# Query, key and value units: seven block products in place of eight, with the block sums on GpSimd

## The chip, the core and the metric

The kernel runs on one NeuronCore of a Trainium2 chip. The core has a matrix engine (TensorE, PE in the profile, with its weight loads as PEld), three engines for elementwise work (VectorE or DVE, ScalarE or ACT, GpSimd or POOL), a queue engine that mainly issues transfers (SyncE, SP) and 16 DMA engines between HBM and the on-chip memory SBUF. Matrix products are collected in eight banks of PSUM, a second on-chip memory. The metric is the device time of one execution in microseconds (us). Lower is better.

## What is computed

One layer of a streaming encoder on 512 tokens of width 1024, all in float32. The change touches the queries, keys and values:

```python
def reference(x, norm_mix_g, w_in, ...):
        xn = rmsnorm(h, norm_mix_g[l])
        proj = xn @ w_in[l]
        zu, zv, q, k, va, ga, gb = jnp.split(proj, split_idx, axis=-1)
        u = jax.nn.gelu(zu, approximate=False)
        v = jax.nn.gelu(zv, approximate=False)
        y_a = gmlp_spatial_gating(u, v, ...) @ w_branch_a[l]
        att = sliding_window_attention(q..., k..., va..., attn_sinks[l])
        y_b = att @ w_branch_b[l]
        gates = jax.nn.sigmoid(jnp.concatenate([ga, gb], axis=-1) + gate_bias[l])
        h = h + (g_a * y_a + g_b * y_b) @ w_out[l]
        hn = rmsnorm(h, norm_ffn_g[l])
        h = h + hierarchical_moe(hn, ...)
    return rmsnorm(h, norm_final_g)
```

`q` has 1024 columns, `k` and `va` 256 each: 1536 columns of `w_in`, with a contraction over 1024. Behind the attention and the gating stands a mixture of 32 experts of which each token uses two; the kernel sorts the tokens by expert and streams the weights of all experts from HBM.

## The kernel before

All weights of the first half pass through the core in 34 **units** of 1 MB (`units`). A unit is 256 columns of a weight over the whole contraction (a tall unit: 8 slices of 128 rows, `TALL`) or 512 columns over half of it (a wide unit, 4 slices, `WIDE`). Units 0 to 3 (`ZV`) are wide and give `zv`; units 4 to 9 (`Q` to `ZU`) are tall and give the queries (4 to 7), the keys (8) and the values (9); unit 10 (`ZU`) begins the next part, and the rest follows in the order of the list.

Every product is made with float32 accuracy out of three products of a rounded type (`F32R`): each operand is split in a high part and the rest, and high·high, high·low and low·high are added up in one PSUM bank (`three`, L738 to L742, `wide_unit`, L744 to L773). The path of a unit is:

1. SP issues its load to one of two buffers `raw` (L457 to L462), once the unit two places ahead has been split.
2. ACT copies the 2048 columns of `raw` to `whi` (`split_hi`, L1351 to L1355), two buffers as well. It waits until PE has finished with the unit whose `whi` it overwrites (`wait_unit_used`).
3. DVE subtracts `whi` from `raw` and writes `wlo` (`split_lo`, L1698).
4. PE works through the unit. A tall unit has two tiles (`tall_tile`, L810): 128 columns of the weight are the stationary operand, all 512 tokens of the activation `xnT_hi` or `xnT_lo` the moving one, 8 slices by three products, so 24 matmuls of 128x512 for a tile and 48 for a unit.
5. ACT copies each finished tile out of PSUM to `qT`, `kT` or `vaT` (L1446 to L1449).

The splits run one unit ahead of PE. Each engine has an instruction stream of its own that is written out by hand in the code and is carried out in its order; the streams meet at semaphores (`hi_split`, `lo_split`, `act_tile_done` and others). An instruction that waits holds up all that is behind it in its stream. In the query, key and value units DVE has, besides the splits, the layernorm of `v_tok`: the statistics of all four token tiles and an inverse root in unit 4 (`layernorm_stats`), then one tile in each of units 4 to 7 (`layernorm`). `v_tok` is read by PE behind the first tiles of unit 10. In the wide units DVE also makes the position biases `alibi` (L1708 to L1717) and turned weights `wsT`. GpSimd does nothing between the start (`ident`, `dist_i`) and the end of the attention.

Behind the first half the expert weights are loaded in place of buffers that PE has finished with; SP waits for PE or DVE before each of these loads.

## Time and profile before

| | |
|---|---|
| Time, median of 3 runs | 893.21 us |
| Lowest and highest of them | 892.12 and 893.25 us |
| The profiled execution's own time | 892.7 us |
| Its span, first to last instruction | 890.8 us |
| PE busy | 840.9 us, 94% of the span |
| DVE busy | 418.4 us, 47% |
| ACT busy | 238.4 us, 27% |
| POOL busy | 7.0 us, 1% |
| Mean granted TensorE clock | 0.981 |
| Query, key and value units | 59.1 to 124.4 us |

All rows come from one profiled execution; its time is 0.5 us below the median of the three runs. A row of a timeline gives the start from the span's first instruction, the duration, engine and line, what is written and read, the shape, and in brackets how long the engine was idle just before and for whom. Matmuls are pipelined: a duration covers also the way through the array, and what one costs in a dense stream is the distance from its start to the next one's. The same holds, to a smaller degree, for DVE and ACT: a row of 0.68 us may be followed by the next one 0.60 us after its start. "PEclk" is the share of the full TensorE clock that was granted.

### The profile page before, as it was taken

Reading aid. Unit: us, or ns where it says so; the run is one execution under the profiler, and the core shown is the slowest. Engines: PE = TensorE matmul, PEld = TensorE weight load, DVE = VectorE, ACT = ScalarE, POOL = GpSimd, SP = SyncE. Lnnn points to the kernel's source line nnn. Section 1 sums busy time; section 2 is a strip of 40 time slices with the busy share of each in tenths; the row PEclk is TensorE's granted clock in tenths of the full one; section 3 lists DMA queues with packets and bytes.
Section 4 is the critical chain, followed back from the end, with each engine's and each line's share of the span. In section 5 each row is a group of like instructions: output and inputs, shape, how many; then the busy total and the mean of one; then the engine's idle time right before and its main releaser. Section 6 shows DMA issues by size and latency. Waiting matters only on the chain.

```text
span 890.8 us, 11444 instructions
## 1 busy us (share of the span) xinstructions
PE 840.9 (94%) x4631; PEld 550.5 (62%) x4631; DVE 418.4 (47%) x814; ACT 238.4 (27%) x439; POOL 7.0 (1%) x24
## 2 busy tenths in 40 slices
PE   8999999999999999999999969999995699999985
PEld 7888888887877888888734333544532353644632
DVE  5538326777765344433868245135133224335134
ACT  6332222465453222224414211110110100100114
POOL 0000000000000100000000000000000000000000
PEclk9999999999999999999999989999996899999998
DMA  8544312212123733796899999999999999999994
GB/s 295 147 94 108 103 59 94 96 48 95 61 83 78 214 95 95 264 402 235 349 379 390 415 430 425 428 426 430 424 429 427 426 428 428 427 427 426 427 410 182
DMA packets 71751, 249.49 MB, mean 280 GB/s; under 512 B 23016, under 2 KB 46608, under 8 KB 58512
## 3 DMA queue, kind: packets, MB, share of 16 engines
q1 hardware_dynamic: 71328, 247.66, 71.5%
q0 software_dynamic: 288, 1.05, 0.3%
q8 instruction: 38, 0.62, 0.3%
q14 instruction: 17, 0.14, 0.0%
q10 hardware_dynamic: 80, 0.02, 0.0%
HBM read 244.51 MB, written 4.20 MB: 279 GB/s over the span
## 4 chain that ended last, share of the span: by engine, by line
PE 85%; DMA 11%; DVE 2%; ACT 1%; issue 1%; SPq 0%; DVEq 0%; POOL 0%; ACTq 0%; POOLq 0%
PE bank L1065 17%; PE bank L740 10%; PE bank L742 10%; PE bank L741 10%; PE bank L1124 8%; DMA R<-w_down 6%; DMA R<-w_up 3%; PE bank L769 2%; PE bank L768 2%; PE bank L767 2%; DMA R<-w_gate 2%; PE bank L1029 2%; PE by_side L1029 2%; PE bank L1152 2%; PE bank L1111 2%; PE bank L1153 1%
## 5 line engine op out<-in xcount | busy, mean ns | idle before, releaser
L1065 PE MATMUL bank<-R,packT 128*64 128x512 f32 (+1 forms) x972 | 184.4, 603 | 15.3 <-DMA R<-w_up 12.8
L1065 PEld LDWEIGHTS bank<-R,packT 128*64 128x64 f32 (+1 forms) x972 | 58.3, 128 | 123.4 <-issue 122.9
L1698 DVE TENSOR_TENSOR wlo<-raw,whi 128x2048 fp32r<-128x2048 f32 x33 | 75.5, 2288 | 84.8 <-ACT whi L1355 84.7
L740 PE MATMUL bank<-xnT_hi,whi 128*128 128x512 f32 x288 | 113.2, 393 | 0.0
L742 PE MATMUL bank<-xnT_hi,wlo 128*128 128x512 f32 x288 | 112.1, 389 | 0.0
L741 PE MATMUL bank<-xnT_lo,whi 128*128 128x512 f32 x288 | 112.1, 389 | 0.0
L1124 PE MATMUL bank<-R,actT 128*64 128x512 f32 (+1 forms) x384 | 74.8, 640 | 14.9 <-DMA R<-w_down 14.7
L1355 ACT ACTIVATE whi<-raw 128x2048 fp32r<-128x2048 f32 x33 | 63.1, 1912 | 67.4 <-PE by_side L742 33.8
L740 PEld LDWEIGHTS bank<-xnT_hi,whi 128*128 128x128 f32 x288 | 54.1, 188 | 11.4 <-issue 0.6
L742 PEld LDWEIGHTS bank<-xnT_hi,wlo 128*128 128x128 f32 x288 | 54.1, 188 | 11.3
L1124 PEld LDWEIGHTS bank<-R,actT 128*64 128x64 f32 (+1 forms) x384 | 22.7, 135 | 62.0 <-issue 61.3
L741 PEld LDWEIGHTS bank<-xnT_lo,whi 128*128 128x128 f32 x288 | 54.1, 188 | 10.9
L2196 DVE SCALAR_TENSOR_TENSOR y_lo<-bank,small,y_hi 128x512 fp32r<-128x512 f32 x26 | 19.3, 750 | 82.3 <-ACT y_hi L1573 82.3
L2205 DVE TENSOR_TENSOR h_tok<-bank,h_tok 128x512 f32<-128x512 f32 x84 | 52.1, 676 | 6.9 <-PE bank L1153 6.9
L1573 ACT ACTIVATE y_hi<-bank,small 128x512 fp32r<-128x512 f32 x26 | 17.8, 690 | 107.0 <-PE bank L1124 91.7
L2182 DVE TENSOR_REDUCE small<-bank 128x1 f32<-128x512 f32 x13 | 9.0, 690 | 72.1 <-PE bank L1082 72.0
L2188 DVE TENSOR_TENSOR act_rows<-silu_g,bank 128x512 f32<-128x512 f32 x13 | 14.0, 1078 | 60.8 <-PE bank L1065 60.8
L1568 ACT ACTIVATE actT<-by_side 128x512 f32<-128x512 f32 x13 | 7.8, 600 | 119.0 <-PE by_side L1089 119.0
L1152 PE MATMUL bank<-y_hi,onehotT 128*128 128x512 f32 x84 | 35.0, 417 | 1.5 <-ACT packT L1554 1.5
L1153 PE MATMUL bank<-y_lo,onehotT 128*128 128x512 f32 x84 | 33.0, 392 | 0.0
L1382 ACT ACTIVATE probs<-probs,small 128x128 f32<-128x128 f32 (+1 forms) x64 | 24.4, 386 | 23.1 <-DVE small L1766 23.1
L1560 ACT ACTIVATE silu_g<-bank 128x512 f32<-128x512 f32 x12 | 7.1, 596 | 82.5 <-PE bank L1065 82.5
(418 smaller groups left out, 1323.4 us busy)
## 6 DMA issues: line engine op xcount, KB each, us to landing
R<-w_up SPq DMA_DIRECT2D x27, 2048.0 KB, 20.7
R<-w_gate SPq DMA_DIRECT2D x25, 2048.0 KB, 22.5
R<-w_down SPq DMA_DIRECT2D x21, 2048.0 KB, 24.4
raw<-w_in SPq DMA_DIRECT2D x17, 1024.0 KB, 5.1
R<-w_down SPq DMA_DIRECT2D x12, 1024.0 KB, 14.2
R<-w_gate SPq DMA_DIRECT2D x14, 512.0 KB, 8.5
raw<-w_in SPq DMA_DIRECT2D x20, 256.0 KB, 4.6
R<-w_up SPq DMA_DIRECT2D x5, 1024.0 KB, 8.3
```

The source lines that it names most:

```text
L740: pe.matmul(dst, hi_w, hi_x, start=start, stop=False)
L741: pe.matmul(dst, hi_w, lo_x, start=False, stop=False)
L742: return pe.matmul(dst, lo_w, hi_x, start=False, stop=stop)
L1029: mm = pe.matmul(bank[PACK_BANKS[c // 2]][:, (c % 2) * 2 * P:(c % 2 + 1) * 2 * P], part[:, t, c, :], onehot[:, t, :], start=(t == 0 and pa ...
L1065: mm = pe.matmul(dst[s * w:(s + 1) * w, :], packT[:, side, c, s * w:(s + 1) * w], part_of(s, c) if part_of else slots[s // 2].tiles[s % 2] ...
L1124: mm = pe.matmul(bank[5 + n][s * w:(s + 1) * w, :], actT[:, c, s * w:(s + 1) * w], slots[s // 2].tiles[s % 2][:, c * D + n * 512:c * D + ( ...
L1152: pe.matmul(dst, onehotT[odd][:, t * P:(t + 1) * P], y_hi[:, n * 512:(n + 1) * 512], start=True, stop=False)
L1153: pe.matmul(dst, onehotT[odd][:, t * P:(t + 1) * P], y_lo[:, n * 512:(n + 1) * 512], start=False, stop=True).then_inc(line.spread_done, 1)
L1355: act.activation(whi[c % 2][:, :], raw[c % 2][:, :], ACT.Copy).then_inc(hi_split, 1)
L1382: act.activation(row, row, ACT.Exp, bias=neg_max[s % 2][:, r:r + 1], accum_out=denom[s % 2][:, r:r + 1])
L1698: dve.tensor_tensor(wlo[c % 2][:, :], raw[c % 2][:, :], whi[c % 2][:, :].bitcast(F32), ALU.subtract).then_inc(lo_split, 1)
L2205: dve.tensor_tensor(part, bank[spread_banks(line, i)[n][t]][:, :], part, ALU.add).then_inc(line.h_added, 1)
```

## The change

The six units 4 to 9 are computed by the Winograd form of Strassen's identity, with a two by two partition of each product: the 1024 deep contraction is halved (4 slices each), the unit's 256 columns are two halves of 128, and the 512 tokens two halves of 256. In place of eight block products of 128 columns by 4 slices by 256 tokens there are seven (`seventh`), on sums of blocks. A block is 12 matmuls of 128x256; a unit has 84 of them (`seven_unit`), the six units 504, where 288 of 128x512 stood.

- **Sums of the activation**: `tT_sum` 0, 1 and 3 are made once by GpSimd in seven additions or subtractions of 128x1024, one behind the other; `tT_sum` 2 by DVE in three. ACT and DVE split the four of them (`tT_hi`, `tT_lo`).
- **Sums of the weights**: for each unit GpSimd makes four sums of 128x512 (`s_sum`), in order s1 to s4, as soon as the unit is loaded. For units from the third on they also wait until the unit two ahead is split.
- **Splits**: in place of one split of 2048 columns there are seven of 512 (`high_block` on ACT, `low_block` on DVE), three of them of blocks of `raw` and four of sums. They go to a ring of eight places made of the same `whi` and `wlo`; block q waits until PE has finished block q - 8. The last two have places of their own (`late_hi`, `late_lo`). SP loads a unit once all seven blocks of the one two ahead are split.
- **Results**: partial sums in PSUM serve two or more results. ACT copies three of them out of PSUM (`keep`), DVE makes three quarters of the result by adding a kept part to a bank (`add_corner`), ACT copies the fourth. Block 2 of a unit waits for the first copy of ACT, block 4 for the third, block 6 for the second `add_corner` of DVE.
- **Order**: the layernorm statistics are made in units 0 and 1 of the six (two token tiles each, the inverse root in unit 1), the layernorm's four tiles in units 2 to 5. The split of unit 10 stands in unit 5.

The rest is renumbering of waits, and semaphores that are merged (`pool_made`, `small_ready`).

```diff
+        RAW_BLOCK = {0: (0, 0), 3: (0, 1), 6: (1, 1)}
+        SUM_BLOCK = {1: 0, 2: 1, 4: 2, 5: 3}
...
+        def block_home(u, b, ring, late):
+            q = 7 * u + b
+            home = late[q - BLOCKS + 2][:, :] if q >= BLOCKS - 2 else ring[q % 8 // 4][:, q % 4 * 512:(q % 4 + 1) * 512]
+            return home.rearrange("p (k n) -> p k n", k=4)
...
             def load_unit(c):
                 if c >= 2:
-                    sp.wait_ge(hi_split, c - 1)
-                    sp.wait_ge(lo_split, c - 1)
+                    sp.wait_ge(hi_split, units_split(c - 2))
+                    sp.wait_ge(lo_split, units_split(c - 2))
                 for dst, src in units[c]:
...
+            pool.wait_ge(xnT_ready, X_READY)
+            minus(t1, hi(0, 1), hi(0, 0)).then_inc(pool_made, 1)
+            minus(tT_part[0][:, :, :], lo(0, 1), lo(0, 0)).then_inc(pool_made, 1)
+            pool.wait_ge(pool_made, T_SUMS + 2)
+            pool.tensor_tensor(t1, t1, tT_part[0][:, :, :], ALU.add).then_inc(pool_made, 1)
...
+            for u in range(SEVENS):
+                c = Q + u
+                if u == 1:
+                    pool.wait_ge(xnT_ready, X_READY + 3 + 4)
+                pool.wait_ge(unit_loaded[c % 2], landed[c])
+                if u >= 2:
+                    pool.wait_ge(lo_split, Q + 7 * (u - 1))
+                s1, s2, s3, s4 = (tile[:, :, :] for tile in s_sum[u % 2])
+                pool.tensor_tensor(s1, raw_block(c, 1, 0), raw_block(c, 1, 1), ALU.add).then_inc(pool_made, 1)
+                pool.wait_ge(pool_made, S_SUMS + 4 * u + 1)
+                minus(s2, s1, raw_block(c, 0, 0)).then_inc(pool_made, 1)
+                minus(s3, raw_block(c, 0, 0), raw_block(c, 1, 0)).then_inc(pool_made, 1)
+                pool.wait_ge(pool_made, S_SUMS + 4 * u + 2)
+                minus(s4, raw_block(c, 0, 1), s2).then_inc(pool_made, 1)
...
-            for c in range(Q, ZU):
-                for m in range(2):
-                    act_tile(c, m, 8 + 2 * (c - Q) + m)
+            def seventh(u, b, dst, x_hi, x_lo, start):
+
+                pe.wait_ge(lo_split, Q + 7 * u + b + 1)
+                w_h, w_l = block_home(u, b, whi, late_hi), block_home(u, b, wlo, late_lo)
+                for k in range(4):
+                    pe.matmul(dst, w_h[:, k, :], x_hi[:, k, :], start=start and k == 0, stop=False, skip_group_check=True)
+                    pe.matmul(dst, w_h[:, k, :], x_lo[:, k, :], start=False, stop=False, skip_group_check=True)
+                    mm = pe.matmul(dst, w_l[:, k, :], x_hi[:, k, :], start=False, stop=k == 3, skip_group_check=True)
+                mm.then_inc(act_tile_done, 1)
+
+            def seven_unit(u):
+
+                main_psum, first_psum, fifth_psum = (bank[2 * i + u % 2][:, 0:2 * P] for i in range(3))
+                if u < 2:
+                    pe.wait_ge(act_tile_read, 5 + u)
+                else:
+                    pe.wait_ge(act_tile_read, 8 + 2 * (u - 1))
+                    pe.wait_ge(corner_ready, 3 * (u - 1))
+                seventh(u, 0, main_psum, x_block(xnT_hi, 0, 0), x_block(xnT_lo, 0, 0), True)
+                pe.wait_ge(xnT_ready, X_READY + 3 + 1)
+                seventh(u, 1, fifth_psum, tT_hi[0], tT_lo[0], True)
+                pe.wait_ge(part_kept, 3 * u + 1)
+                pe.wait_ge(xnT_ready, X_READY + 3 + 2)
+                seventh(u, 2, main_psum, tT_hi[1], tT_lo[1], False)
+                if u < 2:
+                    pe.wait_ge(act_tile_read, 7 + u)
+                seventh(u, 3, first_psum, x_block(xnT_hi, 1, 0), x_block(xnT_lo, 1, 0), True)
+                pe.wait_ge(part_kept, 3 * u + 3)
+                pe.wait_ge(xnT_ready, X_READY + 3 + 3)
+                seventh(u, 4, main_psum, tT_hi[2], tT_lo[2], False)
+                seventh(u, 5, fifth_psum, x_block(xnT_hi, 1, 1), x_block(xnT_lo, 1, 1), False)
+                pe.wait_ge(corner_ready, 3 * u + 2)
+                pe.wait_ge(xnT_ready, X_READY + 3 + 4)
+                seventh(u, 6, main_psum, tT_hi[3], tT_lo[3], False)
+
+            for u in range(SEVENS):
+                seven_unit(u)
...
+            def high_block(u, b):
+                q = 7 * u + b
+                if q < 4:
+                    wait_unit_used(act, 2)
+                elif q < 8:
+                    act.wait_ge(act_tile_done, 8)
+                elif q < BLOCKS - 2:
+                    act.wait_ge(act_tile_done, 8 + q - 7)
+                if b in RAW_BLOCK:
+                    act.wait_ge(unit_loaded[u % 2], landed[Q + u])
+                else:
+                    act.wait_ge(pool_made, S_SUMS + 4 * u + SUM_BLOCK[b] + 1)
+                act.activation(block_home(u, b, whi, late_hi), block_source(u, b), ACT.Copy).then_inc(hi_split, 1)
+
+            def keep(u, i, b, src):
+                act.wait_ge(act_tile_done, 8 + 7 * u + b + 1)
+                return act.activation(kept[u % 2][i][:, :], src[:, 0:2 * P], ACT.Copy)
...
+                if c == Q - 1:
+                    high_t(0, pool_made, T_SUMS + 3)
+                    high_t(1, pool_made, T_SUMS + 5)
+                    high_t(2, xnT_ready, X_READY + 3)
+                    for b in range(4):
+                        high_block(0, b)
...
+            high_block(0, 4)
+            high_block(0, 5)
+            high_t(3, pool_made, T_SUMS + 7)
+            high_block(0, 6)
+            act.wait_ge(wsT_psum, 1)
+            for u in range(SEVENS):
+                last = u == SEVENS - 1
+                main_psum, fifth_psum = bank[u % 2], bank[4 + u % 2]
+                if not last:
+                    high_block(u + 1, 0)
+                keep(u, 0, 0, main_psum).then_inc(part_kept, 1)
+                if last:
+                    split_hi(ZU)
+                else:
+                    high_block(u + 1, 1)
+                keep(u, 1, 1, fifth_psum).then_inc(part_kept, 1)
+                if not last:
+                    high_block(u + 1, 2)
+                keep(u, 2, 2, main_psum).then_inc(part_kept, 1)
+                if not last:
+                    for b in range(3, 7):
+                        high_block(u + 1, b)
+                act.wait_ge(act_tile_done, 8 + 7 * u + 7)
+                act.activation(corner(u, 1, 0), main_psum[:, 0:2 * P], ACT.Copy).then_inc(act_tile_read, 2)
...
+            def low_block(u, b):
+                dve.wait_ge(hi_split, Q + 7 * u + b + 1)
+                lo = dve.tensor_tensor(block_home(u, b, wlo, late_lo), block_source(u, b),
+                                       block_home(u, b, whi, late_hi).bitcast(F32), ALU.subtract)
+                lo.then_inc(lo_split, 1)
+
+            def add_corner(u, m, h, b, src, i):
+                dve.wait_ge(act_tile_done, 8 + 7 * u + b + 1)
+                dve.wait_ge(part_kept, 3 * u + i + 1)
+                dve.tensor_tensor(corner(u, m, h), src[:, 0:2 * P], kept[u % 2][i][:, :], ALU.add).then_inc(corner_ready, 1)
...
+                if c == Q - 1:
+                    for i in range(3):
+                        low_t(i)
+                    for b in range(6):
+                        low_block(0, b)
+                    low_t(3)
+                    low_block(0, 6)
...
+            for u in range(SEVENS):
+                last = u == SEVENS - 1
+                main_psum, first_psum, fifth_psum = bank[u % 2], bank[2 + u % 2], bank[4 + u % 2]
+                if not last:
+                    low_block(u + 1, 0)
+                    low_block(u + 1, 1)
+                else:
+                    split_lo(ZU)
+                if u < 2:
+                    layernorm_stats(2 * u)
+                else:
+                    layernorm(u - 2)
+                if not last:
+                    low_block(u + 1, 2)
+                    low_block(u + 1, 3)
+                add_corner(u, 0, 0, 3, first_psum, 0)
+                if not last:
+                    low_block(u + 1, 4)
+                add_corner(u, 1, 1, 4, main_psum, 1)
+                if not last:
+                    low_block(u + 1, 5)
+                add_corner(u, 0, 1, 5, fifth_psum, 2)
+                if not last:
+                    low_block(u + 1, 6)
```

The orders of the built programs show it at four places. First TensorE in a middle unit: before, triples of 128x512 with the normed activation `xnT` as moving operand.

```order
L742 MATMUL bank<-xnT_hi,wlo_75 128x512
L740 MATMUL bank<-xnT_hi,whi_73 128x512
L741 MATMUL bank<-xnT_lo,whi_73 128x512
L742 MATMUL bank<-xnT_hi,wlo_75 128x512
L740 MATMUL bank<-xnT_hi,whi_73 128x512
```

Now the end of one block and the beginning of the next, with the sums of activations (`tT`) in place of `xnT`.

```order
L972 MATMUL by_side<-tT_hi_93,whi_73 128x256
L973 MATMUL by_side<-tT_lo_97,whi_73 128x256
L974 MATMUL by_side<-tT_hi_93,wlo_75 128x256
L972 MATMUL bank<-tT_hi_94,whi_73 128x256
L973 MATMUL bank<-tT_lo_98,whi_73 128x256
L974 MATMUL bank<-tT_hi_94,wlo_75 128x256
```

Each matmul has half the columns, and the bank changes behind 12 of them.

Second ScalarE, from the end of the wide units on; `v_tok` is the Gelu of the tiles of `zv`, `whi` a high part, `qT` a result. Before:

```order
L1436 ACTIVATE v_tok<-bank 128x512 x3
L1436 ACTIVATE v_tok<-by_side 128x512
L1355 ACTIVATE whi_73<-raw_71 128x2048
L1449 ACTIVATE qT<-bank 128x512 x2
L1355 ACTIVATE whi_72<-raw_70 128x2048
```

And now, in the piece that begins three instructions behind those Gelus (the high parts of blocks 4 and 5 stand between):

```order
L1543 ACTIVATE tT_hi_96<-tT_sum_104 128x1024
L1557 ACTIVATE whi_73<-raw_70 128x512
L1557 ACTIVATE whi_73<-raw_71 128x512
L1561 ACTIVATE kept_115<-bank 128x256
L1557 ACTIVATE whi_72<-s_sum_111 128x512
L1561 ACTIVATE kept_116<-by_side 128x256
L1557 ACTIVATE whi_72<-s_sum_112 128x512
L1561 ACTIVATE kept_117<-bank 128x256
```

The first copy of a partial sum (`kept_115`) stands behind the remaining splits of unit 0 and the first one of unit 1.

Third VectorE in its layernorm work. Before, with the split of a whole unit between two tiles:

```order
L1733 TENSOR_SCALAR v_tok<-v_tok,small 128x1024
L1734 TENSOR_TENSOR v_tok<-v_tok,ln_g 128x1024
L1735 TENSOR_TENSOR v_tok<-v_tok,ln_b 128x1024
L1698 TENSOR_TENSOR wlo_74<-raw_70,whi_72 128x2048
L1733 TENSOR_SCALAR v_tok<-v_tok,small 128x1024
```

Now, unit 2 of the six (`qT<-bank,kept_116` is the addition that block 6 waits for):

```order
L1983 TENSOR_TENSOR wlo_75<-s_sum_111,whi_73 128x512
L1886 TENSOR_SCALAR v_tok<-v_tok,small 128x1024
L1887 TENSOR_TENSOR v_tok<-v_tok,ln_g 128x1024
L1888 TENSOR_TENSOR v_tok<-v_tok,ln_b 128x1024
L1983 TENSOR_TENSOR wlo_75<-s_sum_112,whi_73 128x512
L1983 TENSOR_TENSOR wlo_74<-raw_71,whi_72 128x512
L1990 TENSOR_TENSOR qT<-bank,kept_115 128x256
L1983 TENSOR_TENSOR wlo_74<-s_sum_113,whi_72 128x512
L1990 TENSOR_TENSOR qT<-bank,kept_116 128x256
```

The addition on which PE waits stands behind a layernorm tile, three splits and another addition. In unit 1 the statistics of two tiles and the inverse root stand where the layernorm tile is here.

Fourth GpSimd behind `dist_i`; before, its next work was `row_iota`, behind the attention.

```order
L704 IOTA dist_i 128x128
L707 TENSOR_TENSOR tT_sum_101<-xnT_hi 128x1024
L707 TENSOR_TENSOR tT_part_105<-xnT_lo 128x1024
L715 TENSOR_TENSOR tT_sum_101<-tT_sum_101,tT_part_105 128x1024
L707 TENSOR_TENSOR tT_sum_102<-xnT_hi,tT_sum_101 128x1024
L719 TENSOR_TENSOR tT_sum_102<-tT_sum_102,xnT_lo 128x1024
L707 TENSOR_TENSOR tT_sum_104<-xnT_hi,tT_sum_102 128x1024
L723 TENSOR_TENSOR tT_sum_104<-tT_sum_104,xnT_lo 128x1024
L732 TENSOR_TENSOR s_sum_107<-raw_70 128x512
```

Seven instructions of 128x1024 and 24 of 128x512 stand where there was nothing.

## Rows read from the trace of the kernel before

**Rows 1.** The page: the chain that ended last, by engine.

```profile
PE 85%; DMA 11%; DVE 2%; ACT 1%; issue 1%; SPq 0%; DVEq 0%; POOL 0%; ACTq 0%; POOLq 0%
```

**Rows 2.** Busy time by stretch: the six units (columns: PE, PEld, DVE, ACT, POOL).

```profile
59.12:124.40 65.28, 65.28 (x290) 54.07 (x288) 34.32 (x42) 18.00 (x18) 0.00 (x0) 1.00 0.33 97
```

**Rows 3.** Timeline of PE: first matmuls of unit 4 and of unit 10.

```profile
59.12 0.39 PE L740 MATMUL bank<-xnT_hi,whi 128*128 128x512 f32 x1
...
124.40 0.39 PE L740 MATMUL bank<-xnT_hi,whi 128*128 128x512 f32 x1
```

**Rows 4.** Timeline of PE: second and last of 64 matmuls of 128x256 (`gather_rows`).

```profile
565.41 0.28 PE L1029 MATMUL bank<-onehot,hn_lo 128*128 128x256 f32 x1
...
572.84 0.28 PE L1029 MATMUL by_side<-onehot,hn_lo 128*128 128x256 f32 x1
```

**Rows 5.** Timeline of ACT: copies by size, the last Gelu of `zv`.

```profile
4.48 1.06 ACT L1391 ACTIVATE xn_tok<-x_tok 128x1024 f32<-128x1024 f32 x1 [0.51 <-DMA x_tok<-x]
...
7.23 2.57 ACT L1401 ACTIVATE whi<-raw 128x512 fp32r<-128x512 f32 x4
10.30 0.47 ACT L1407 ACTIVATE xnT_hi<-by_side,small 128x256 fp32r<-128x256 f32 x1 [0.49 <-PE bank L725]
...
59.32 0.60 ACT L1436 ACTIVATE v_tok<-by_side 128x512 f32<-128x512 f32 x1 [2.12 <-PE by_side L769]
```

**Rows 6.** Timeline of DVE: low parts of 256 and 512 columns.

```profile
10.81 0.48 DVE L1801 SCALAR_TENSOR_TENSOR xnT_lo<-by_side,small,xnT_hi 128x256 fp32r<-128x256 f32 x1 [0.72 <-ACT xnT_hi L1407]
11.21 0.68 DVE L1795 TENSOR_TENSOR wlo<-raw,whi 128x512 fp32r<-128x512 f32 x1
11.81 0.48 DVE L1801 SCALAR_TENSOR_TENSOR xnT_lo<-bank,small,xnT_hi 128x256 fp32r<-128x256 f32 x1
```

**Rows 7.** Timeline of DVE: statistics, inverse root and one tile of the layernorm.

```profile
67.08 1.29 DVE L1724 BATCH_NORM_STATS2 small<-v_tok 128x6 f32<-128x512 f32 x2
...
70.21 0.17 DVE L1728 COPY small<-small 128x4 f32<-128x4 f32 x1
...
72.60 0.81 DVE L1733 TENSOR_SCALAR v_tok<-v_tok,small 128x1024 f32<-128x1024 f32 x1
...
75.85 2.28 DVE L1698 TENSOR_TENSOR wlo<-raw,whi 128x2048 fp32r<-128x2048 f32 x1
```

**Rows 8.** Timelines of POOL and DVE around 291 us.

```profile
291.38 1.40 POOL L683 TENSOR_SCALAR_AFFINE_SELECT earlier<-all_ones 128x128 bf16<-128x128 bf16 x1
...
290.33 2.29 DVE L1698 TENSOR_TENSOR wlo<-raw,whi 128x2048 fp32r<-128x2048 f32 x1 [0.53 <-ACT whi L1355]
```

**Rows 9.** POOL by form: a read with DVE idle, and iotas of two sizes.

```profile
L658 POOL TENSOR_SCALAR_AFFINE_SELECT ident<-ident 128x128 f32<-128x128 f32 x1 | 0.3, 287 | 0.2 <-POOL ident L656 0.2
...
L664 POOL IOTA row_iota<- 128x256 f32 x1 | 0.4, 351 | 288.1 <-DVE attT_lo L1775 288.1
...
L661 POOL IOTA dist_i<- 128x128 int32 x1 | 0.2, 230 | 0.0
```

**Rows 10.** Timeline of DVE from 27 us; timeline of PE at wide unit 2.

```profile
27.98 2.97 DVE L1715 TENSOR_SCALAR alibi<-dist 64x128 f32<-64x128 f32 x16
...
31.19 2.29 DVE L1698 TENSOR_TENSOR wlo<-raw,whi 128x2048 fp32r<-128x2048 f32 x1
...
37.26 0.48 PE L767 MATMUL bank<-whi,xnT_hi 128*128 128x512 f32 x1
```

**Rows 11.** Timeline of PE: two waits and the work behind them, then the granted clock.

```profile
446.45 0.64 PE L1065 MATMUL bank<-gate_fifth,packT 128*64 128x512 f32 x1 [1.35 <-DVE packT L2213]
...
678.48 9.03 PE L1065 MATMUL bank<-R,packT 128*32 128x512 f32 x64 [11.91 <-DMA R<-w_up]
...
444.00:446.00 2.00, 1.11 (x6) 1.00 0.02 6
678.00:680.00 2.00, 1.52 (x8) 0.50 0.98 418
```

**Rows 12.** A wait of the SP queue in front of expert weights' loads.

```profile
SPq L526 <- PE by_side L769: 25.3, 1, 25.3
```

133 lines of the change are left out of this document (87 added, 46 removed).

## The prediction

> **What bounds the kernel now.** I read the chain that ended last first: PE is 85% of it and DVE 2% [rows 1], so what counts is whether PE is given work. The busy times by stretch say the same of the six units: from 59.12 to 124.40 PE is busy for all of the 65.28 us, DVE for 34.32, ACT for 18.00, POOL for none, and the granted clock is 1.00 [rows 2]. The reader is to see there that the stage is dense on PE, and that the other engines run beside it with room. Units 4 to 9 cost 124.40 - 59.12 = 65.28 us on the path, 10.88 a unit, 65.28 / 288 = 0.2267 us for a matmul of 512 columns [rows 3]. Later loads wait for PE or DVE [rows 12]: no transfer of the expert weights starts at a fixed time, each follows a buffer that was finished with. So what is won or lost before 124.4 us is carried to the end one to one.
>
> **What is removed and added on PE.** Removed are 288 x 0.2267 = 65.3 us. Added are 504 matmuls of 256 columns. The trace has such a stream: 62 distances from 565.41 to 572.84 are 7.43 us, 0.120 each [rows 4], with a weight load of 128 columns before each of them as in the new code. That is 504 x 0.120 = 60.5 us, 10.08 a unit, 1.44 a block. PE's own work shrinks by **4.8 us**. It is not half of 0.2267 because each matmul has some 0.013 us that do not shrink (0.120 x 2 - 0.2267).
>
> **What the other engines now have to do in 10.08 us.** Prices: ACT, high part of 512 columns 2.57 / 4 = 0.64, of 1024 columns 1.06, a copy of 256 out of PSUM 0.47 [rows 5]. DVE, low part of 512 columns 0.60 (11.21 to 11.81), an operation on 256 columns with a bank 0.40, or 0.48 to its end [rows 6]; statistics of two token tiles 70.21 - 67.08 = 3.13; inverse root 72.60 - 70.21 = 2.39; a layernorm tile 75.85 - 72.60 = 3.25 [rows 7]. ACT has 7 x 0.64 + 4 x 0.47 = 6.4 us a unit, and fits. DVE has 7 x 0.60 + 3 x 0.40 = 5.4, with a layernorm tile 8.7, with statistics and root 10.9. The sum of a unit fits in most of them, but PE waits in the middle: block 6 is due 6 x 1.44 = 8.64 us into a unit and needs DVE's second addition, and the order puts the layernorm before it. I lay the streams side by side, counting from the unit's start on PE; a block's result is there 0.16 after its end (0.28 - 0.12 in [rows 4]).
>
> - Units 2 to 4. DVE can begin the low part of the next unit's block 1 at 2.8: block 0 ends at 1.44 + 0.16, ACT then keeps its copy and makes the high part. From there low part 0.60, layernorm 3.25, two low parts 1.20, addition 0.40, low part 0.60, addition 0.48: done at 9.3. PE waits 0.65 in each of the three: **2.0 us**.
> - Unit 1. In place of 3.25 stand 3.13 + 2.39 = 5.52: **2.9 us**.
> - Unit 5. No low parts of a next unit, but the whole split of unit 10: ACT ends its high part at 4.0, DVE 2.20, layernorm 3.25, two additions 0.88: done at 10.3, **1.7 us**.
> - Unit 0. Its first copy stands on ACT behind the last Gelu (starts at 59.32 [rows 5]), four high parts of 512 and one of 1024: 0.54 + 4 x 0.62 + 1.0 + 0.47 = 4.5, so 63.8 where block 2 is due at 59.12 + 2.88 = 62.0: 1.9 us (0.62 being the distance of starts). Then DVE, which gets its low parts late by that, has 3.13 of statistics in its chain and is 2.2 late for blocks 4 and 6: **4.1 us** in all.
>
> These waits are 2.0 + 2.9 + 1.7 + 4.1 = 10.7 us. They swallow the 4.8: **+5.9 us** before GpSimd has cost anything.
>
> **GpSimd.** No row of before shows a two-input operation of it. From below its price is DVE's for the same shape, 0.60 for 512 columns [rows 6]. From above, its one-input select of 128x128, 0.287 us, four times: 1.15, and 2.3 for 1024 [rows 9]. From the two iotas, 0.23 and 0.351, a column costs 0.95 ns and the start 0.11; with two reads for a write I take twice that slope, 1.1 for 512 and 2.1 to 2.2 for 1024, near the upper end, since the select reads as well and an iota does not. By itself this hides: seven sums from 27.2 end at 43, unit 4's four at 47, and ACT wants the first of them only when PE is through with the `whi` of wide unit 2, at 37.3 + 48 x 0.2267 = 48.2 [rows 10]. The question is what happens when both engines read SBUF.
>
> There the trace has one row that decides for me. The select at 291.38 took 1.40 us, where its like took 0.29; a DVE split with two SBUF inputs ran from 290.33 to 292.62, in its usual 2.29, and the select ended just behind it [rows 8, 9]. So the GpSimd read stood still until DVE's instruction was through. Bounds for the cost of this: nothing, if DVE always goes first and GpSimd's work fits in the gaps; or every GpSimd instruction in front of a DVE instruction, the full price each time. I take turns: who asks waits for the one that runs, then they alternate. In unit 1 two of GpSimd's four sums come into DVE's chain, 2 x 1.1 = 2.2. In unit 0 two come into it, and the start is 1 us later since the seven sums, held up by DVE's work between 31 and 48, end near 49: 3.1. In units 2 to 4 the sums start late in the unit, as the load waits for the seven splits two units ahead, so some two of 1.1 fall into the chain in all three: 2.3. Sum 7.6 us.
>
> The Trainium skill, page "SBUF — State Buffer", section "Who interferes with whom", says that a DVE instruction with two SBUF inputs contends with a GpSimd one that reads SBUF, and that the first to issue keeps the shared ports for its whole instruction. By that rule, which also speaks against the change, the waits on DVE's side are as real as the one in [rows 8], which agrees with it on GpSimd's side; no row of before shows DVE waiting. The skill's "GPSIMD Engine Reference", section 3.1, gives 4497 ns for an addition of 2048 columns; a quarter of it, 1.12 us, is an estimate for a weight sum, and the sum above would be the same by it.
>
> **Clock.** Behind a wait of 1.35 us the granted clock stays 1.00, behind one of 11.91 it is 0.50 [rows 11], and the 64 matmuls there take 9.03 us where the same 64 take some 7.1. The waits here reach 4 to 5 us, between the two, so 0 to 2 us; I take 1.
>
> **Sum**, against the profiled execution's 892.7: -4.8 + 10.7 + 7.6 + 1 = +14.5, so 907.2; the median of the runs is 0.5 above that execution: **907.7 us**.
>
> **Rivals.**
> 1. *GpSimd costs DVE nothing* (DVE always goes first, or the two only share). For it: the DVE split in [rows 8] was not lengthened. Against it: there DVE had begun first. Then -4.8 + 10.7: 892.7 + 5.9 + 0.5 = **899.1**.
> 2. *The turns begin at once.* At 27.15 DVE enters a run of some 20 short operations on the biases, ahead of the split of unit 2 [rows 10], and GpSimd gets its seven long sums at the same moment. If each short one has to let a sum of 2.2 pass, the split that ends at 33.5 now ends at 33.5 + 7 x 2.2 = 48.9, and PE, which wants it at 37.3, waits 11.5 us. Against it: those operations have one input, and no row tells whether such a one meets GpSimd. Saved is little, since the later sums are then early. Sum 907.7 + 11.5 = **919**, with the clock's second us 920.
> 3. *The other side: the waits do not come.* It decides where DVE's second addition is done before 8.64. In units 2 to 4 that takes 0.65 us less of chain, in unit 1 2.9 less, for instance if DVE's starts come closer than the rows say and it enters each unit with its low parts already made. Then PE keeps its 4.8: 893.2 - 4.8 = **888.4**. Against it: all prices are of this trace, and the low part of block 1 cannot be made before block 0 of the running unit has left the ring. A half of it gives no change.
> 4. *The matmuls of 256 columns do not run at 0.120*, since each needs a load of new weights, which takes 0.19 in the rows of PEld. [Rows 4] has a new load each time too. It would cost up to 504 x 0.07 = 35 us; I give it 2 in 100.
>
> **Chances.** Forecast 0.48 (turns with another rule of precedence move it between 904 and 914), rival 1 0.20, rival 2 0.20, rival 3 0.07, no change 0.03, rival 4 0.02. The range goes from rival 1 with a us to spare, 898, to rival 2 at 920. A difference of 0.2% is 1.8 us, about what a measurement of this kernel tells from no change: faster 0.07, same 0.03, slower 0.90.
>
> **What will show it.** In the profile after: distances of 0.120 us between PE's new matmuls in dense stretches; block 6 idle for DVE's addition in every unit, longest in units 0 and 1; block 2 of unit 0 idle for ACT's copy. Rows of 128x512 low parts that take 1 us and more while GpSimd's sums run would show the turns, and unchanged 0.68 us would speak for rival 1. PE idle before unit 2 of the wide ones would be rival 2. Unit 10 should start near 138 us; from there all should be as before, later by the same amount. I am wrong if GpSimd's sums of 512 columns are far from 1.1 us, or if the expert stage takes up the delay.

## The result: 42 us slower, three times the forecast

| | before | after |
|---|---|---|
| Median of 4 runs each | 893.23 us | 935.44 us |
| Lowest and highest | 892.12, 893.50 | 934.51, 935.75 |
| Span of the profiled execution | 890.8 us | 933.8 us |
| First matmul of unit 4 (seven unit 0) | 59.12 us | 72.62 us |
| First matmul of unit 10 | 124.40 us | 166.3 us |
| First matmul of the expert stage | 441.5 us | 483.4 us |

The ratio is 1.0477, 95% interval 1.0464 to 1.0489. The forecast was 907.7 in 898 to 920: the sign was right, the size not. Unit 10 and the expert stage are both 41.9 us late and the span is 43.0 longer, so the loss arises before 166 us and is carried on, as the prediction had it.

The page of after, busy times and the chain that ended last. Against [rows 1] PE fell from 85% of the chain to 74% and DVE rose from 2% to 10%:

```profile
PE 852.3 (91%) x4847; PEld 567.3 (61%) x4847; DVE 481.2 (52%) x875; ACT 256.3 (27%) x491; POOL 65.1 (7%) x55
...
PE 74%; DMA 11%; DVE 10%; issue 2%; ACT 2%; SPq 0%; DVEq 0%; ACTq 0%
```

The stretch that answers to [rows 2] (columns: PE, PEld, DVE, ACT, POOL busy, then the granted clock). PE works for 71 of 94 us, at 0.87 of its clock, where it was busy throughout at 1.00:

```profile
72.62:166.32 93.70, 71.14 (x506) 69.51 (x505) 71.15 (x94) 33.18 (x64) 33.10 (x20) 0.87 0.29 79
```

Timeline of PE in after: the first two of the new matmuls, 0.12 apart as in [rows 4], and then all rows up to unit 10 that have a wait above 1 us. The first wait stands before wide unit 2, where [rows 10] has a start at 37.26:

```profile
72.62 0.28 PE L972 MATMUL bank<-xnT_hi,whi 128*128 128x256 f32 x1
72.74 0.28 PE L973 MATMUL bank<-xnT_lo,whi 128*128 128x256 f32 x1
...
48.09 0.79 PE L843 MATMUL bank<-whi,xnT_hi 128*128 128x512 f32 x1 [10.71 <-DVE wlo L1849]
...
76.77 0.38 PE L972 MATMUL bank<-tT_hi,whi 128*128 128x256 f32 x1 [1.11 <-ACT kept L1561]
...
81.17 0.39 PE L972 MATMUL bank<-tT_hi,whi 128*128 128x256 f32 x1 [1.27 <-ACT kept L1561]
...
88.13 0.58 PE L972 MATMUL bank<-tT_hi,whi 128*128 128x256 f32 x1 [3.83 <-DVE qT L1990]
...
106.51 0.58 PE L972 MATMUL bank<-tT_hi,whi 128*128 128x256 f32 x1 [6.65 <-DVE qT L1990]
...
123.28 0.58 PE L972 MATMUL bank<-tT_hi,whi 128*128 128x256 f32 x1 [4.13 <-DVE qT L1990]
...
140.21 0.58 PE L972 MATMUL bank<-tT_hi,whi 128*128 128x256 f32 x1 [4.15 <-DVE qT L1990]
...
164.79 0.38 PE L972 MATMUL bank<-tT_hi,late_hi 128*128 128x256 f32 x1 [1.31 <-DVE vaT L1990]
```

The rows of 3.83, 6.65, 4.13 and 4.15 us are block 6 of units 0 to 3, waiting for DVE's second addition. From one of them to the next is one unit, 10.08 us without losses: 106.51 - 88.13 = 18.38 = 10.08 + 6.65 + 1.65, and 123.28 - 106.51 = 16.77 = 10.08 + 4.13 + 2.56. The third part is 0.16 of refilling and otherwise the clock, which the windows show (last columns: granted clock, DMA, GB/s). It reads 1.00 in the first part of the wait, 0.74 from 104 to 106, where PE is still idle, and 0.50 to 0.55 from 106 to 112:

```profile
100.00:104.00 4.00, 0.00 (x0) 0.00 (x0) 3.73 (x9) 0.52 (x1) 2.86 (x3) 1.00 0.00 0
104.00:108.00 4.00, 1.49 (x7) 1.49 (x8) 3.98 (x8) 0.00 (x0) 0.00 (x0) 0.62 0.00 0
108.00:112.00 4.00, 4.00 (x21) 4.00 (x21) 0.69 (x1) 0.91 (x2) 0.00 (x0) 0.53 0.70 222
```

The balance up to unit 10: matmuls -4.8; start 13.5 (72.62 - 59.12: 10.7 of wait, 2.7 of half clock behind it); waits in the units 1.11 + 1.27 + 3.83 + 6.65 + 4.13 + 4.15 + 1.31 and a quarter us in unit 4 = 22.7, with 0.16 of refilling for each (0.28 of duration less 0.12 of distance, [rows 4]) some 1.2 more; half clock behind the four long ones 1.5 + 2.4 + 2.6 + 2.6 = 9.1. The sum is 41.7 of the 41.9.

What DVE and GpSimd did at the start, timelines of after. Against [rows 10], the sixteen multiplications of the biases (`alibi`) take 13.37 us in place of 2.97, and two short operations ahead of them 2.40 each, the length of one of GpSimd's sums. Of the sixteen only five are held, one for each sum that is still to come (2.27 to 2.38 us); the one behind each of these, and all six behind the last sum, take 0.21 to 0.23. So the delay is as long as the sums that run, not one sum for every short operation. The split for wide unit 2 begins at 45.74 in place of 31.19:

```profile
27.26 2.40 DVE L1860 TENSOR_SCALAR dist<-dist 64x128 f32<-64x128 f32 x1
29.69 2.40 DVE L1861 SCALAR_TENSOR_TENSOR dist<-dist 128x128 f32<-128x128 f32 x1
32.13 13.37 DVE L1866 TENSOR_SCALAR alibi<-dist 64x128 f32<-64x128 f32 x16
...
45.74 2.29 DVE L1849 TENSOR_TENSOR wlo<-raw,whi 128x2048 fp32r<-128x2048 f32 x1
...
27.18 2.40 POOL L707 TENSOR_TENSOR tT_sum<-xnT_hi 128x1024 f32<-128x1024 f32 x1 [25.46 <-DVE xnT_lo L1973]
...
41.82 2.34 POOL L723 TENSOR_TENSOR tT_sum<-tT_sum,xnT_lo 128x1024 f32<-128x1024 f32 x1
```

The same in unit 1, where DVE makes the inverse root out of operations on four columns. Those that fall beside one of GpSimd's sums (97.74 to 102.86, 1.26 to 1.30 each) take 1.14 to 1.29 us, their likes 0.16. The statistics (BATCH_NORM_STATS2) are not held: those at 80.59 and 82.14, beside sums too, kept 1.27 and 1.29.

```profile
97.57 0.17 DVE L1837 TENSOR_SCALAR small<-small 128x4 f32<-128x4 f32 x1
97.77 1.29 DVE L1838 TENSOR_SCALAR small<-small 128x4 int32<-128x4 int32 x1
99.10 0.16 DVE L1841 TENSOR_TENSOR small<-small 128x4 f32<-128x4 f32 x1
99.30 1.14 DVE L1842 SCALAR_TENSOR_TENSOR small<-small 128x4 f32<-128x4 f32 x1
...
97.74 1.30 POOL L732 TENSOR_TENSOR s_sum<-raw 128x512 f32<-128x512 f32 x1 [7.18 <-DMA raw<-w_in]
99.12 1.30 POOL L707 TENSOR_TENSOR s_sum<-s_sum,raw 128x512 f32<-128x512 f32 x1
```

Low parts of 512 columns take 1.4 to 1.8 us where they meet a sum, 0.68 where not. Unit 2 has, ahead of the addition on which block 6 waits, a pass of the layernorm and three low parts that are held:

```profile
115.65 2.20 DVE L1888 TENSOR_TENSOR v_tok<-v_tok,ln_b 128x1024 f32<-128x1024 f32 x1
117.78 1.78 DVE L1983 TENSOR_TENSOR wlo<-s_sum,whi 128x512 fp32r<-128x512 f32 x1
119.48 1.75 DVE L1983 TENSOR_TENSOR wlo<-raw,whi 128x512 fp32r<-128x512 f32 x1
...
121.48 1.41 DVE L1983 TENSOR_TENSOR wlo<-s_sum,whi 128x512 fp32r<-128x512 f32 x1
```

Over their lengths alone (1.23 and 0.68) that is 3.9 us.

### The profile page after: what moved, and what is told of

Read it like the earlier page. It is cut to its first block, busy times and chain, and to the rows that moved or that the text cites. A ratio compares the mean times of both kernels' runs of the same rounds, so it can differ in the third digit from the quotient of the medians.

```text
span 933.8 us, 12110 instructions
## 1 busy us (share of the span) xinstructions
PE 852.3 (91%) x4847; PEld 567.3 (61%) x4847; DVE 481.2 (52%) x875; ACT 256.3 (27%) x491; POOL 65.1 (7%) x55
## 3 DMA queue, kind: packets, MB, share of 16 engines
q0 software_dynamic: 288, 1.05, 0.3%
## 4 chain that ended last, share of the span: by engine, by line
PE 74%; DMA 11%; DVE 10%; issue 2%; ACT 2%; SPq 0%; DVEq 0%; ACTq 0%
PE bank L1176 16%; PE bank L816 7%; PE bank L817 7%; PE bank L818 7%; PE bank L1235 6%; DMA R<-w_down 5%; DMA R<-w_gate 3%; DMA R<-w_up 3%; PE bank L843 2%; PE bank L844 2%; PE bank L845 2%; PE bank L1140 2%; PE by_side L1140 2%; DVE wlo L1983 2%; PE bank L1222 2%
## 5 line engine op out<-in xcount | busy, mean ns | idle before, releaser
L1849 DVE TENSOR_TENSOR wlo<-raw,whi 128x2048 fp32r<-128x2048 f32 x27 | 61.8, 2287 | 49.6 <-ACT whi L1466 49.6
L816 PE MATMUL bank<-xnT_hi,whi 128*128 128x512 f32 x192 | 75.9, 395 | 0.0
L818 PE MATMUL bank<-xnT_hi,wlo 128*128 128x512 f32 x192 | 74.8, 390 | 0.0
L817 PE MATMUL bank<-xnT_lo,whi 128*128 128x512 f32 x192 | 74.8, 389 | 0.0
L1466 ACT ACTIVATE whi<-raw 128x2048 fp32r<-128x2048 f32 x27 | 51.6, 1911 | 60.3 <-PE by_side L818 33.8
L1235 PEld LDWEIGHTS bank<-R,actT 128*64 128x64 f32 (+1 forms) x384 | 22.7, 135 | 61.0 <-issue 60.3
L972 PE MATMUL bank<-tT_hi,whi 128*128 128x256 f32 x80 | 25.8, 323 | 21.2 <-DVE qT L1990 18.8
L816 PEld LDWEIGHTS bank<-xnT_hi,whi 128*128 128x128 f32 x192 | 36.1, 188 | 7.6 <-issue 0.6
L818 PEld LDWEIGHTS bank<-xnT_hi,wlo 128*128 128x128 f32 x192 | 36.0, 188 | 7.6
L817 PEld LDWEIGHTS bank<-xnT_lo,whi 128*128 128x128 f32 x192 | 36.1, 188 | 7.0
L972 PEld LDWEIGHTS bank<-tT_hi,whi 128*128 128x128 f32 x80 | 17.5, 219 | 22.7 <-DVE qT L1990 19.6
```

What stands on the lines that cost most here:

```text
L816: pe.matmul(dst, hi_w, hi_x, start=start, stop=False)
L817: pe.matmul(dst, hi_w, lo_x, start=False, stop=False)
L818: return pe.matmul(dst, lo_w, hi_x, start=False, stop=stop)
L972: pe.matmul(dst, w_h[:, k, :], x_hi[:, k, :], start=start and k == 0, stop=False, skip_group_check=True)
L1235: mm = pe.matmul(bank[5 + n][s * w:(s + 1) * w, :], actT[:, c, s * w:(s + 1) * w], slots[s // 2].tiles[s % 2][:, c * D + n * 512:c * D + ( ...
L1466: act.activation(whi[c % 2][:, :], raw[c % 2][:, :], ACT.Copy).then_inc(hi_split, 1)
```

## The experiments

The theory after this reading (A): an instruction of GpSimd and one of DVE take turns, one whole instruction each, short ones of DVE too. Against it stood that the delays come from the change's longer instruction lists, from their order, or from the placing of the data.

### 1. The same sums in the kernel before

In the kernel before, seven additions whose results nothing uses:

```diff
+            pool.wait_ge(xnT_ready, WIDE + KT)
+            for n in range(7):
+                pool.wait_ge(iota_made, n + 1)
+                pool.tensor_tensor(spare.rearrange("p (k n) -> p k n", k=4), xnT_hi[:, 0:4, 0:256].bitcast(F32),
+                                   xnT_lo[:, 0:4, 0:256].bitcast(F32), ALU.add).then_inc(iota_made, 1)
```

> The kernel before, with seven two-input additions of 128x1024 float32 added on GpSimd behind the normalised activation (from 27 us), whose results nothing uses; the matmuls and all else are those of before. Theory A (turns): VectorE's sixteen alibi multiplications take 13 us in place of 2.97, TensorE waits 10 to 11 us for the low part of unit 2 and runs 2 to 3 us at half clock after it: 893.2 + 13.5 = 906.7, range 904 to 908. Theory B (the delay belongs to something else in the change): 893.2, within 1.

Measured: 906.99 us (905.74 to 907.96, ratio 1.0153, interval 1.0136 to 1.0171), +14.1. The timelines of DVE and PE, and a window, have the rows of after again, in a kernel in which nothing else of DVE's and PE's work is changed; the second row is the summary of the sixteen (ns: shortest, median, longest):

```profile
32.26 13.37 DVE L1722 TENSOR_SCALAR alibi<-dist 64x128 f32<-64x128 f32 x16
...
L1722 DVE TENSOR_SCALAR alibi<-dist x16: 209/220/2372, 32.3 to 45.4; 64x128 f32<-64x128 f32 x16
...
48.21 0.80 PE L774 MATMUL bank<-whi,xnT_hi 128*128 128x512 f32 x1 [10.82 <-DVE wlo L1705]
...
50.00:54.00 4.00, 4.00 (x11) 3.05 (x10) 2.30 (x2) 0.00 (x0) 0.00 (x0) 0.50 1.28 238
```

Theory A holds for the start in the time and in the cause: 14 us of the 42 are seven sums of GpSimd that meet a run of short operations. Its turns are not strictly one for one: the median of the sixteen is 0.22, so most of them pass unheld.

### 2. Instructions that only write

The same place, but fourteen iotas of 1024 columns into the spare tile (`pool.iota` for `pool.tensor_tensor` above).

> The kernel before, with fourteen instructions on GpSimd that only write 128x1024 float32 (ascending numbers, no input from memory) in the same place, from 27 us, whose results nothing uses. Theory A1 (the turns are for reading two operands): no alibi row above 0.3 us, 893.2 within 1. Theory A2 (any GpSimd instruction that touches the core's memory takes turns with VectorE): sixteen alibi multiplications at one GpSimd instruction each; with instructions of 1 us or more these take at least 12 us, and the time is above 902.

Measured: 897.76 us (894.41 to 899.25), ratio 1.0060. Neither expectation is right. Timelines of GpSimd and DVE:

```profile
27.10 14.72 POOL L668 IOTA spare<- 128x1024 f32 x14 [25.38 <-DVE xnT_lo L1827]
...
27.20 0.97 DVE L1716 TENSOR_SCALAR dist<-dist 64x128 f32<-64x128 f32 x1
28.20 0.29 DVE L1717 SCALAR_TENSOR_TENSOR dist<-dist 128x128 f32<-128x128 f32 x1
28.53 8.16 DVE L1722 TENSOR_SCALAR alibi<-dist 64x128 f32<-64x128 f32 x16
...
37.66 2.29 DVE L1705 TENSOR_TENSOR wlo<-raw,whi 128x2048 fp32r<-128x2048 f32 x1
```

The multiplications with one input are held by an instruction that only writes (8.16 us in place of 2.97, an iota being 14.72 / 14 = 1.05). They pass in pairs, one pair for each iota, and a single one lasts 0.62 to 0.98; the second expectation had put one iota to each of the sixteen. The operations with two inputs, L1717 and the split, are not: 0.29 and 2.29, their usual lengths. Beside sums L1717's like took 2.40 (L1861 in after). So a two-input operation of DVE meets GpSimd's reads, and a one-input TENSOR_SCALAR also its writes. The profiled execution had a wait of 2.70 us on PE and the clock at 1.00 behind it, at 894.4; two of the other runs took 899, and why is open.

### 3. Which of DVE's instructions are held

In the kernel before, fourteen sums as in the first experiment, but from 134 us on (`pool.wait_ge(gate_used, 1)`), where DVE gates the tiles of the next stage.

> The kernel before, with fourteen additions of 128x1024 float32 on GpSimd whose results nothing uses, beginning when VectorE has used the first gate (near 134.5 us, in the matmuls of unit 10), where VectorE's rows have several kinds of operands: gated from a bank of PSUM and the biases (0.69 us), gated from two tiles (0.69), a one-input cast (0.43), the low part (0.69), the split of a unit (2.28). Theory A (turns, whole instructions; and by the trace of the changed kernel instructions with an operand in PSUM are not held): the rows with an operand in PSUM stay at 0.69, the other four kinds take up to 2.4 us more each while the sums run; the sums are 14 x 2.35 = 33 us of which VectorE's idle time (5.6 of 12.7 us for two tiles) takes in some 20, so that TensorE waits some 13 us for the gated tiles, with 2 to 5 us of half clock: 905 to 912. Theory D (only the many short instructions at 27 us are held, longer ones are not): all these rows keep their length, 893.

Measured: 907.63 us (906.21 to 908.69), as theory A has it, with three waits of PE (3.44, 6.01, 1.03), though for the splits and not for gated tiles. DVE's rows from 134.79, each one beside sums:

```profile
134.79 2.76 DVE L1874 TENSOR_TENSOR spT_lo<-gated,spT_hi 128x512 fp32r<-128x512 f32 x1
137.48 4.45 DVE L1705 TENSOR_TENSOR wlo<-raw,whi 128x2048 fp32r<-128x2048 f32 x1
141.85 0.68 DVE L1868 TENSOR_TENSOR gated<-bank,gate_bs 128x512 f32<-128x512 f32 x1
142.56 2.14 DVE L1871 TENSOR_TENSOR gated<-gbuf,gated 128x512 f32<-128x512 f32 x1
144.74 2.50 DVE L1873 CAST spT_hi<-gated 128x512 fp32r<-128x512 f32 x1
...
134.38 41.28 POOL L668 TENSOR_TENSOR spare<-xnT_hi,xnT_lo 128x1024 f32<-128x1024 f32 x14 [132.66 <-DVE gated L1871]
```

The addition with one operand in PSUM keeps its 0.68. The others, of 0.69, 2.29, 0.69 and 0.43 us alone, take 1.45 to 2.16 us more each, at most one sum. The sums pay too: 41.28 / 14 = 2.95 in place of 2.35.

The Trainium skill, page "SBUF — State Buffer", section "Who interferes with whom", has these cases: two SBUF inputs contend with a GpSimd instruction that reads, not with one that only writes; a copy, cast or `tensor_scalar` can contend in a mode with two ports; one SBUF input outside these modes does not. The rows of this and the last experiment agree with it, and so do the statistics above; which mode an instruction ran in no row shows. The prediction took from that section only the part on two inputs; the part on `tensor_scalar` speaks for its rival 2.

### 4. The changed kernel with later activation sums

```diff
             pool.wait_ge(xnT_ready, X_READY)
+            pool.wait_ge(lo_split, units_split(2))
```

> The changed kernel with one wait more: GpSimd begins its seven 1024-column sums of the activation only when VectorE has split unit 2, so that they run from about 34 to 51 us, behind VectorE's sixteen alibi multiplications and not beside them. Theory A (an instruction of GpSimd that reads two operands and an instruction of VectorE take turns, one whole instruction each): the 16 alibi rows take 2.97 us in place of 13.37, TensorE's unit 2 begins near 37.3 and not 48.1, and the 10.8 us of wait and the 2.7 us of half clock behind it go: 935.4 - 13.5 = 921.9, range 920 to 926 since the sums now end nearer to their use. Theory B (VectorE is late for another reason that the change brought, as its own longer list of work or another placing of the tiles): the alibi rows stay at 13.37 us and the time stays at 935.4, within 1.

Measured: 926.19 us (924.12 to 927.46), just above theory A's range and far from theory B. The biases are back at 2.97 us, and PE does not wait before wide unit 2. But only 9.2 of the 13.5 us are won. The sums now meet other work of DVE, and PE begins seven unit 0 with a wait (timelines of DVE and PE):

```profile
43.33 3.41 DVE L2001 TENSOR_TENSOR tT_sum<-xnT_hi 128x1024 f32<-128x1024 f32 x1
...
63.05 0.55 PE L973 MATMUL bank<-xnT_hi,whi 128*128 128x256 f32 x1 [3.36 <-DVE wlo L1984]
```

### 5. Without weight sums, and without any sums

Two kernels that leave sums out. In the first the weights' sums are missing from the kernel of experiment 4, in the second all of GpSimd's sums from the changed kernel (one-element writes stand in their place). Neither computes the layer any more.

```diff
-                pool.tensor_tensor(s1, raw_block(c, 1, 0), raw_block(c, 1, 1), ALU.add).then_inc(pool_made, 1)
-                minus(s2, s1, raw_block(c, 0, 0)).then_inc(pool_made, 1)
...
+                for s in (s1, s2, s3, s4):
+                    pool.memset(s[:, 0:1, 0:1], 0.0).then_inc(pool_made, 1)
```

> The kernel late_sums with the weights' block sums (128x512, four a unit) left out and the activation's (128x1024) kept, so the output is not that of the reference. It parts what late_sums still loses: the wait of 3.4 us at unit 0's beginning, with its half clock, belongs to the activation's sums, which keep VectorE's three own sums at 3.4 in place of 1.22 us; the waits in units 0 to 3 to the weights' sums. Then: no_sums 898.3 + 3.4 + 1.5 = 903, range 900 to 906. If the waits in the units came from elsewhere than these sums, 915 or more.

Measured: 897.74 us (896.91 to 899.18). The weights' sums are worth 926.2 - 897.7 = 28.5 us. My expectation was 5 too high, and the time lies below its range, because I had put the wait at 63 us to the activation's sums. It is gone here, though these are still made and DVE's own sums still take 3.4 us each: what had delayed the first low parts were the weights' sums from 55.65 on.

> The changed kernel with GpSimd's sums left out: each of its instructions of sums writes one element only, and the splits read a tile of the activation or of the raw weights where a sum stood; every other instruction (504 matmuls of 256 columns, copies, splits, additions, their order and waits) is unchanged, so the output is not that of the reference. Theory A (turns between GpSimd and VectorE): all that is left is the shorter matmuls, -4.8, and the waits that ScalarE's and VectorE's orders make without GpSimd, +10.7, with 1 to 3 us of clock: 893.2 - 4.8 + 10.7 + 1 to 3 = 900 to 902; no VectorE row of 512 columns above 0.70 us. Theory C (the waits of the seven-product units come from the order of VectorE's instructions alone, GpSimd only moved the start): the start is cured, 13.5 us, and the rest stays: 921.9.

Measured: 898.34 us (898.08 to 898.93), ratio 1.0060, a little under the 900 to 902 of theory A and far from theory C. So the sums on GpSimd cost 935.4 - 898.3 = 37.1 us: 14.1 at the start (experiment 1), and the rest, 23.0, in the units. This division holds for the changed kernel only: with the start cured, the weights' sums alone were worth 28.5. What remains is the change without its sums, still 5.5 us slower than before. Timeline of PE, its waits above 1 us:

```profile
63.14 0.39 PE L963 MATMUL bank<-tT_hi,whi 128*128 128x256 f32 x1 [1.11 <-ACT kept L1552]
...
70.50 0.39 PE L963 MATMUL bank<-tT_hi,whi 128*128 128x256 f32 x1 [1.34 <-DVE qT L1981]
...
83.34 0.38 PE L963 MATMUL bank<-tT_hi,whi 128*128 128x256 f32 x1 [2.51 <-DVE qT L1981]
```

With 1.31 in unit 5 and 0.24 twice, PE waits 6.7 us, 7.7 with refilling, and runs at 0.60 of its clock from 84 to 88 us; unit 10 begins at 129.4, 5.0 later than before: -4.8 + 7.7 + some 2 of clock.

Leaving the sums out takes away two things, the turns and the time in which a split waits for its sum. The rows of after tell them apart. Ahead of block 6 of units 1, 2 and 3 DVE's held operations are 4.2, 3.9 and 4.0 us longer than their likes. PE's waits there exceed this kernel's (2.51, none and 0.24) by nearly the same: 4.1, 4.1 and 3.9. So in these units it is the turns.

### 6. The order of DVE's work

DVE's layernorm pieces go behind the three additions of each unit, in three kernels: that of experiment 4, the one without sums, and the changed one.

```diff
             for u in range(SEVENS):
...
-                if u < 2:
-                    layernorm_stats(2 * u)
-                else:
-                    layernorm(u - 2)
...
                 if not last:
                     low_block(u + 1, 6)
+                if u < 2:
+                    layernorm_stats(2 * u)
+                else:
+                    layernorm(u - 2)
```

> The kernel late_sums, with VectorE's layernorm pieces (statistics, inverse root, the three passes over the token rows) moved in each unit from before the three additions to behind them. In late_sums TensorE waits 3.8, 6.5, 4.1 and 4.1 us in units 0 to 3 for the second addition. Theory O (order: the addition is late because it stands behind the layernorm piece in VectorE's queue): these waits fall below 1 us each, and with the half clock behind them some 25 us go: below 905. Theory W (work: VectorE's and GpSimd's own two-operand work may not overlap, and a unit's 7 splits of 0.68, 3 additions of 0.41, 4 sums of 1.27 and 3.3 us of layernorm are 14.4 us against 10.1 us of matmuls): the order only decides which unit pays; over six units some 74 us stand against 60.5 and what VectorE is ahead by, so at least 10 us of wait stay, now also for low parts, with half clock: 914 to 926.

Measured: 906.37 us (905.99 to 910.16), 19.8 less than in the old order, and just above theory O's bound. Theory W is wrong that order only moves the waits about, and its 914 was too high. The six units now take 137.0 - 62.4 = 74.6 us. That meets its 74 us of shared work by luck: some 5 of them are half clock, DVE stands idle for 5 of the last 34, and in the kernel `reordered` below the units take 145.7 - 72.8 = 72.9. In the old order they took 157.5 - 63.05 = 94.5, because PE waited for additions that stood behind work without a deadline. Of the four waits for the second addition one long one is left, where theory O had all below 1 us (timeline of PE):

```profile
71.98 0.39 PE L973 MATMUL bank<-tT_hi,whi 128*128 128x256 f32 x1 [2.09 <-ACT kept L1562]
...
103.04 0.58 PE L973 MATMUL bank<-tT_hi,whi 128*128 128x256 f32 x1 [5.64 <-DVE qT L1991]
```

> The changed kernel with one thing moved: VectorE's layernorm pieces stand behind the three additions of each unit and no longer before them; GpSimd's sums begin at 27 us as in the change. Theory O (order, from the pair late_sums and late_reordered, 926.2 to 906.4): the start keeps its 10.8 us of wait and 2.7 us of half clock, the waits for the second addition in units 0 to 3 go down from 18.8 us by some 13 and the half clock behind them by some 6: 935.4 - 19.8 = 915.6, range 913 to 919. If the gain of late_reordered came from VectorE being ahead because the start was cured, little comes here: above 925.

Measured: 915.85 us (915.67 to 916.50), as theory O had it from the pair before. So of the change's 42 us almost 20 go by moving four lines, with the sums where they were.

> The kernel no_sums (GpSimd's sums left out, the splits read other data, so the output is not that of the reference), with VectorE's layernorm pieces behind the three additions of each unit. In no_sums TensorE still waits 1.3 and 2.5 us for the second addition in units 0 and 1, 0.2 twice, with about 1.7 us of half clock; that is order, if the order theory holds where nothing is shared: 898.3 - 1.3 - 2.5 - 0.5 - 1.7 - 0.6 = 891.7, range 890 to 893, a gain of 1 to 3 us on the kernel before, which is what seven products would bring if the sums were free. If the waits there are of another kind (ScalarE's copies late), it stays at 898.

Measured: 890.28 us (median of 11, 889.87 to 891.78), ratio 0.9978, interval 0.9969 to 0.9987. Two waits are left, 1.11 and 0.57; unit 10 begins at 121.6: -4.8 + 1.7 + 0.3 = -2.8. By the medians the gain is 2.0 us. That is what seven products give when GpSimd's sums are free.

Between the two reordered kernels, 906.4 and 890.3, lie 16 us that GpSimd's sums cost in this order. They are not shown to be a floor. The wait of 5.64 stands behind two tiles of statistics and the inverse root in one piece (89.0 to 98.2, four of its small operations held), ahead of unit 2's low parts, and no run with GpSimd's sums spreads that piece.

### 7. The sums on VectorE

GpSimd makes no sums. DVE makes them all; the biases move behind unit 10, the layernorm behind the additions and is written with two passes for three.

```diff
+                    s_sums(u + 1, 0)
                     low_block(u + 1, 1)
+                    s_sums(u + 1, 1)
...
+                then(dve.scalar_tensor_tensor(out=row, in0=row, scalar=ln_mv[:, 2 * t:2 * t + 1], in1=ln_g[:, :],
+                                              op0=ALU.subtract, op1=ALU.mult))
+                dve.scalar_tensor_tensor(out=row, in0=row, scalar=rstd[:, t:t + 1], in1=ln_b[:, :], op0=ALU.mult,
+                                         op1=ALU.add).then_inc(ln_ready, 1)
```

> The changed kernel with all block sums on VectorE and none on GpSimd (seven more of 128x1024 at 1.22 us and four of 128x512 at 0.68 us in each unit), the alibi multiplications moved behind the gating of unit 11, the layernorm's three passes written as two (2.46 in place of 3.27 us a token tile) and moved behind the additions, three of its four tiles to the end of unit 5. If only sharing with GpSimd was dear, VectorE holds: 7 splits, 4 sums and 3 additions are 8.7 us of a unit's 10.1: -4.8 of matmuls, +1.3 for ScalarE's copy in unit 0, +1.3 at unit 5's end: 891, range 889.5 to 893. If VectorE becomes the bound instead (its 32 us before unit 0 are full, and the layernorm has to end by 7 us into unit 10), TensorE waits for low parts or the layernorm: 895 to 905.

Measured: 895.89 us (894.96 to 897.17), ratio 1.0035, in the range of the second case, but by one long wait and not by DVE as the bound throughout. One wait made most of the difference to the first case, and the window behind its start shows the clock (timeline of PE, window):

```profile
101.36 0.58 PE L939 MATMUL bank<-tT_hi,whi 128*128 128x256 f32 x1 [2.75 <-ACT kept L1528]
...
100.00:104.00 4.00, 2.64 (x12) 2.64 (x13) 3.97 (x8) 2.34 (x6) 0.00 (x0) 0.59 0.02 4
```

ACT's copy was late since it stands behind a high part, which waited for a sum, which stood on DVE behind 5.5 us of statistics and inverse root in one piece (92.7 to 98.2). The next kernel spreads these pieces. It also makes ACT's first copy of unit 0 earlier, each unit's first two sums before its first low part, and one layernorm tile before the split of unit 10 (parts of its difference to the changed kernel):

```diff
+                    layernorm_stats(0)
+                    layernorm_stats(1)
+                    for b in range(4, 6):
                         low_block(0, b)
...
+                if u < 2:
+                    layernorm_stats(2 + u)
+                elif u == 2:
+                    layernorm_root()
```

> The kernel vector_sums with its long pieces spread: statistics of token tiles 0 and 1 before unit 0 (VectorE waited 4.4 us there), tiles 2 and 3 in units 0 and 1, the inverse root in unit 2, the tiles' normalisation in units 4, 5, 5, 5; the next unit's first two sums before its first low part; ScalarE's first copy of unit 0 before its last two splits. In vector_sums TensorE waited 1.1 us in unit 0 for that copy and 2.8 us in unit 3, where 5.5 us of statistics and root in one piece made the next unit's first sum late, with 2.5 us of half clock and 0.16 us of refill for each wait. Theory A: these go: 895.9 - 1.1 - 2.8 - 2.5 - 0.5 = 889.0, range 888 to 891, faster than the kernel before by 0.15 to 0.5%. Theory B (VectorE at 8.7 + 1.5 of 10.1 us a unit is the bound wherever the pieces stand): the waits come back in other units, 893 or more.

Measured: 891.43 us (median of 11, 890.28 to 893.04), against 892.71 for the kernel before beside it: ratio 0.9986, interval 0.9977 to 0.9995. That is between the ranges of theories A and B. The long waits are gone, two short ones are left; which of the four rearrangements did how much no run tells:

```profile
66.27 0.39 PE L939 MATMUL bank<-tT_hi,whi 128*128 128x256 f32 x1 [1.44 <-ACT kept L1528]
...
70.09 0.39 PE L939 MATMUL bank<-tT_hi,whi 128*128 128x256 f32 x1 [0.69 <-DVE qT L2001]
...
L783 PE MATMUL bank<-xnT_hi,whi x192: 389/389/499, 122.2 to 362.3; 128*128 128x512 f32 x192
```

Unit 10 begins at 122.2, 2.2 us earlier than before. This version computes all and is the fastest that does, but by 0.14%, less than the 0.2% that the prediction called its limit of telling. The median lies 2.4 above what theory A gave. Of that 1.5 are on record at unit 10 (892.71 - 2.2 = 890.5 where 889.0 was expected, the two waits being most of it); for the other 0.9 the runs give no row.

## Why the prediction was right and wrong

The step that failed is the start, to which the forecast's sum gave nothing; two terms of the sum were too small besides, the turns in the units and the clock.

- **What bounds the kernel, and that a delay is carried on one to one**: right. 41.9 us at unit 10, 41.9 at the expert stage.
- **PE's own work, -4.8**: right. The pitch was 0.12, and the kernel with no sums in the better order is explained with -4.8. Rival 4 is out.
- **Waits without GpSimd, 10.7 us** (+5.9 net): the mechanism was right, and 898.3 was measured where rival 1's sum was 899.1. That the net came so close is partly luck. The waits are 7.7 us: units 2 to 4 wait 0.24 or nothing in place of 0.65 each, unit 0 2.4 in place of 4.1. Some 2 us of clock, which rival 1 did not have, make up for it.
- **Turns, 7.6 us**: right in kind, half in size. The waits in the units are 23.9 us with refilling in after and 7.7 without sums, so the turns cost 16.2, and with their half clock the 23 of experiment 5. (Two parts of the 7.6 are a tenth off in opposite directions.) I had counted only GpSimd's sums that fall into the chain of low parts, two a unit. The inverse root's operations of 0.16 us were held as well, in unit 1, and passes of the layernorm in units 2 and 3; the additions stand behind them. The sums were also dearer than the 1.1 and 2.1 to 2.2 us taken: 1.26 to 1.30 and 2.34 to 2.42 at their shortest, 1.5 to 2.3 for most of the small ones beside DVE.
- **The start, nothing**: this is the step that failed, by 10.8 us of wait and 2.7 of half clock. The forecast let turns begin in the units and gave 0.20 to rival 2, in which they begin at 27 us; its reason against was that the bias operations have one input. Rows of after and experiment 1 show that it does not protect them. Rival 2's price, 11.5 us, was close to the wait of 10.7, since it counted sums and not short operations. By its sum 919 or 920 came out, and the range ended there.
- **Clock, 1 us**: wrong by eleven, 2.7 at the start and 9.1 in the units. The rows had 1.00 behind a wait of 1.35 us and 0.50 behind 11.91 [rows 11], and I took the middle of 0 to 2 us for all waits of 4 to 5 together, where each of the four long ones cost 1.5 to 2.6. Shorter ones are dear as well: windows of up to 4 us read 1.00 behind waits of 1.44 and 1.57, but 0.61 behind 2.09 and 0.60 behind 2.51. The 2.70 of experiment 2, with 1.00 behind it, is the exception.
- **Rival 3**, the waits do not come: it takes another order of DVE's work and no sums on GpSimd, and then gives 890.3 rather than 888.4.

The sum up to unit 10, as forecast and as measured (us):

| | forecast | measured |
|---|---|---|
| PE's own work | -4.8 | -4.8 |
| Waits without GpSimd | 10.7 | 7.7 |
| Turns in the units | 7.6 | 16.2 |
| Start | 0 | 10.8 |
| Clock | 1 | 11.8 |
| Sum | 14.5 | 41.7 |

## What to carry to other kernels

Work moved to GpSimd is not free when DVE works beside it: a DVE operation on SBUF may wait for one whole instruction of GpSimd, however short it is itself. A run of short operations of DVE ahead of something urgent is the worst company: it grows by the length of nearly every GpSimd instruction that falls into it, here from 3 to 13 us. Where two engines' lists meet at a wait, put work without a deadline behind what the other engine waits for: that alone gave back 20 of 42 us. Price a wait of TensorE with the half clock behind it: in these kernels all waits of 2.09 us and more from 36 to 170 us had it, but one.

## What the runs showed of the hardware

- A held instruction ends only after the running one of the other engine has ended, in both directions. DVE's multiplication of 64x128 took up to 2.4 us beside sums of 128x1024, and one more of 0.21 passed before the next sum; the sums took 2.95 on average beside DVE's longer ones.
- Held beside a reading GpSimd: DVE operations with two SBUF inputs (0.16 to 1.14, 0.69 to 2.76, 2.29 to 4.45), and one-input casts and TENSOR_SCALAR (0.43 to 2.50). Beside iotas the one-input TENSOR_SCALAR was (0.22 to between 0.62 and 0.98), two-input operations were not (0.29 and 2.29). An addition with one operand in PSUM was not (0.68), nor the statistics (1.27).
- GpSimd's addition of two SBUF operands in float32: 1.26 to 1.30 us for 128x512, 2.34 to 2.42 for 128x1024.
- The clock fell to 0.50 behind waits of 2.09, 2.51 and 2.75 us and all longer ones from 36 to 170 us, but not behind one of 2.70 (experiment 2). It cost 1.5 to 2.7 us each time in after, with waits from 3.8 to 10.7 us.
